# One transformer layer on one core: the first choice's expert rows are added to the residual by accumulating transfers instead of by VectorE

## What is computed

```python
def hier_moe(xn, w_rg, b_rg, w_re, b_re, w1, w3, w2):
    ...
    topv, topi = lax.top_k(lg_in, TOP_K_INNER)        # TOP_K_INNER = 2
    w_sel = jax.nn.softmax(topv, axis=-1) * p_sel[:, None]
    ...
    def expert_step(acc, inp):
        w1e, w3e, w2e, ge = inp
        hid = jax.nn.silu(t @ w1e) * (t @ w3e)
        return acc + ge[:, None] * (hid @ w2e), None
    ...

def block(x, mod, s_f0, s_b0, is_grid, p):
    ...
    x = x + g1 * m
    xn = rmsnorm(x, norm_ffn_g) * (1 + sc2) + sh2
    x = x + g2 * hier_moe(xn, w_rg, b_rg, w_re, b_re, w1, w3, w2)
    return x, s_f, s_b

y_prompt = rmsnorm(xp, final_norm_g)
y_sample = rmsnorm(xs, final_norm_g)
```

## Time and profile before

| | before |
|---|---|
| median of 3 runs (lowest to highest) | 709.08 us (708.93 to 710.7) |
| the profiled execution's own time | 708.17 us |
| its span | 706.4 us |
| TensorE busy | 597.8 us (85%) |
| VectorE busy | 311.9 us (44%) |
| ScalarE busy | 140.5 us (20%) |
| GpSimd busy | 145.4 us (21%) |
| start of the first load of the tail (L536) | 675.05 us |
| start of VectorE's first addition in the tail | 681.56 us |

### The profile page before, as it was taken

The page is one execution under the profiler, slowest core; times in us unless marked ns, Lnnn a source line. Parts: engine busy times, 40 slices in busy tenths (PEclk is TensorE's granted clock), DMA queues, the critical chain, the costliest instruction groups (busy, mean ns, idle before and its releaser), DMA issues.

```text
span 706.4 us, 8602 instructions
## 1 busy us (share of the span) xinstructions
PE 597.8 (85%) x3512; PEld 397.4 (56%) x3512; DVE 311.9 (44%) x619; ACT 140.5 (20%) x269; POOL 145.4 (21%) x112
## 2 busy tenths in 40 slices
PE   3799999999999899899999758898888788988800
PEld 3579999888888755444554435454444444544300
DVE  1432238432603246424677636554333434433347
ACT  5334522131322233211111120000000100100012
POOL 0133633333424000010000020232222222321200
PEclk9989999999999999999999559999999999999965
DMA  7985232031230697570006749999999999999484
GB/s 281 387 296 188 68 120 90 30 120 28 92 120 0 206 382 247 216 291 31 30 31 252 325 148 421 421 420 418 422 419 420 418 420 421 420 419 419 200 306 188
DMA packets 47463, 178.87 MB, mean 253 GB/s; under 512 B 5597, under 2 KB 5645, under 8 KB 34749
## 3 DMA queue, kind: packets, MB, share of 16 engines
q1 hardware_dynamic: 39128, 156.03, 55.9%
q0 software_dynamic: 7328, 19.63, 7.7%
q10 hardware_dynamic: 964, 2.63, 1.1%
HBM read 170.37 MB, written 14.19 MB: 261 GB/s over the span
## 4 chain that ended last, share of the span: by engine, by line
PE 60%; DMA 23%; DVE 7%; issue 3%; ACT 2%; POOL 2%; SPq 1%; POOLq 0%; ACTq 0%; DVEq 0%
DMA arena_cd<-expert_in_rows,idx 16%; PE bank L946 9%; PE bank L948 9%; PE bank L947 9%; PE bank L1116 9%; PE bank L1252 6%; DMA ring<-in_w_up_e 4%; PE bank L905 3%; POOL expert_out_rows L625 2%; DVE arena_ab L1334 2%; PE bank L1232 2%; DMA x<-in_x_sample 2%; PE bank L1133 2%; PE bank L1224 1%; DMA ring<-expert_out_rows 1%
## 5 line engine op out<-in xcount | busy, mean ns | idle before, releaser
L1232 PE MATMUL bank<-ring,arena_ab 128*64 128x256 f32 x416 | 96.1, 385 | 4.7 <-issue 2.1
L1236 PE MATMUL bank<-ring,arena_ab 128*64 128x256 f32 x416 | 96.2, 385 | 0.0
L1232 PEld LDWEIGHTS bank<-ring,arena_ab 128*64 128x64 f32 x416 | 57.6, 140 | 49.2 <-issue 20.5
L556 POOL TENSOR_TENSOR w_lo<-ring,w_hi 128x1024 fp32r<-128x1024 f32 x25 | 61.4, 2454 | 112.1 <-ACT w_hi L702 112.1
L625 POOL DMA_INDIRECT expert_out_rows<-arena_ab,row_out x32 | 40.6, 1269 | 191.7 <-DVE arena_ab L1334 191.7
L946 PE MATMUL bank<-xn_hi,w_hi 128*128 128x320 f32 x192 | 61.8, 322 | 3.0 <-DVE xn_lo L1334 2.9
L946 PE MATMUL bank<-w_hi,xn_hi 128*128 128x512 f32 x160 | 62.9, 393 | 0.0
L948 PE MATMUL bank<-w_hi,xn_lo 128*128 128x512 f32 x160 | 62.9, 393 | 0.0
L947 PE MATMUL bank<-w_lo,xn_hi 128*128 128x512 f32 x160 | 62.7, 392 | 0.0
L948 PE MATMUL bank<-xn_hi,w_lo 128*128 128x320 f32 x192 | 60.4, 315 | 0.0
L947 PE MATMUL bank<-xn_lo,w_hi 128*128 128x320 f32 x192 | 60.2, 313 | 0.0
(11 more groups left out here) (239 smaller groups left out, 930.3 us busy)
## 6 DMA issues: line engine op xcount, KB each, us to landing
ring<-in_w_gate_e SPq DMA_DIRECT2D x26, 1024.0 KB, 21.0
ring<-in_w_up_e SPq DMA_DIRECT2D x26, 1024.0 KB, 23.2
ring<-in_w_down_e SPq DMA_DIRECT2D x26, 1024.0 KB, 19.5
ring<-in_w_ada SPq DMA_DIRECT2D x11, 2048.0 KB, 11.2
ring<-in_w_in SPq DMA_DIRECT2D x6, 2048.0 KB, 8.2
arena_ab<-in_w_gate_e SPq DMA_DIRECT2D x6, 1024.0 KB, 21.4
arena_ab<-in_w_up_e SPq DMA_DIRECT2D x6, 1024.0 KB, 23.7
arena_ab<-in_w_down_e SPq DMA_DIRECT2D x6, 1024.0 KB, 19.7
```

What stands on the lines that cost most here:

```text
L556: pool.tensor_tensor(as_piece(w_lo[p_ % 2], p_), piece_of(w, p_), as_piece(w_hi[p_ % 2], p_), ALU.subtract).then_inc(w_lo_ready, 1)
L1232: pe.matmul(bank[2 + p_][0:BLK, 0:DE], lhs, w_gate(s)[:, kt, :], start=(kt == 0), stop=(kt == KT - 1))
L1236: last = pe.matmul(bank[2 + p_][BLK:2 * BLK, 0:DE], lhs, w_up(s)[:, kt, :], start=(kt == 0), stop=(kt == KT - 1))
```

## The change

The plain loads of the first choice's rows are taken out. In their place POOL issues, at the end of its program, five transfers that add the DRAM rows of the first choice to `x` where it lies (`accum_op=ALU.add`), tile by tile, after `y_all`. `got` shrinks to one piece for each tile. VectorE's `combine` waits for the load of the second choice and for the accumulating transfer of the same tile, and does one addition in place of two.

```diff
-        got = flat[:, 0:2 * NT * D].rearrange("p (t j n) -> p t j n", t=NT, j=2)
+        got = flat[:, 0:NT * D].rearrange("p (t n) -> p t n", t=NT)
...
+        first_sum = [sem(f"first_sum{t}") for t in range(NT)]
...
             sp.sem_inc(y_all, 1)
             for t in range(NT):
-                for j in range(2):
-                    sp.dma_start(got[:, t, j, :], y_rows[j * TOK + P * t:j * TOK + P * t + P, :]).then_inc(got_in[t], 16)
+                sp.dma_start(got[:, t, :], y_rows[TOK + P * t:TOK + P * t + P, :]).then_inc(got_in[t], 16)
...
                 pool.wait_ge(idx_ov_ready, 1)
+
+            pool.wait_ge(y_all, 1)
+            for t in range(NT):
+                pool.dma_start(x[:, t, :], y_rows[P * t:P * t + P, :], accum_op=ALU.add).then_inc(first_sum[t], 16)
...
             def combine(t):
 
-                g0, g1 = got[:, t, 0, :], got[:, t, 1, :]
-                dve.wait_ge(got_in[t], 32)
-                then(tt(g0, g0, g1, ALU.add))
-                tt(x[:, t, :], x[:, t, :], g0, ALU.add).then_inc(x2_ready[t], 1)
+                dve.wait_ge(got_in[t], 16)
+                dve.wait_ge(first_sum[t], 16)
+                tt(x[:, t, :], x[:, t, :], got[:, t, :], ALU.add).then_inc(x2_ready[t], 1)
```

## The result

| | before | changed |
|---|---|---|
| median of 9 runs each (lowest to highest) | 708.53 us (706.45 to 710.7) | 711.08 us (710.39 to 714.34) |
| ratio, 95% interval | | 1.0051 (1.0035 to 1.0067) |
| profiled execution, its span | 708.17, 706.4 us | 714.34, 712.5 us |
| start of SP's first load of the tail | 675.05 us | 678.64 us |
| from there to the start of c4's last addition | 21.2 us | 23.7 us |

The changed kernel is slower, by 0.5% by the ratio and by 0.4% by the two medians. Its profiled execution was the slowest of the nine: its tail begins 3.6 us later than that of the kernel before, and the change touches nothing ahead of the tail. The difference of the tails, 33.9 - 31.4 = 2.5 us, is also the difference of the two medians, 711.08 - 708.53 = 2.55.

The account below looks back on a forecast made before the run. VectorE's work was taken to bound the tail, with 4.7 us of transfer slack; dearer sums and a store move c4 from 696.26 to 699.2, +2.9 us on the 709.08 median: 712.0 us, range 705.4 to 718.3.

Parts of the forecast that it names:

- The bound: In the tail, VectorE's own work from c2 on sets the end; transfers have 4.7 us of slack.
- The gain: On VectorE, five additions go; only those of c2, c3 and c4 are on the path, at most 3.7 us.
- f = 2: Price of an accumulating transfer in plain loads, one per tile read; adds 6.3 us, last sum at 697.9; chance 0.36.
- POOL's issues at zero: On POOL, issuing five transfers takes 2.7 to 5.4 us from 675.05, ahead of the data, and costs nothing.
- the counting back: From the last sum at 697.9, pairs land 3.78 us apart, at 682.8, 686.6, 690.3, 694.1 and 697.9.
- The cover that was named: Five plain loads keep the transfer engines busy 6.3 us from 677.9, so late POOL issues cost little until about 684.
- A store among the sums, 1.26 us: n0's store moves its data while the last sums are moved, putting the last landing at 699.2 instead of 697.9.
- What c4 waits for: On VectorE, c4's remaining addition waits for the last accumulating transfer and starts at 699.2, against 696.26 before.
- the sum of +2.9 us: Net effect on the span: c4's addition starts at 699.2 in place of 696.26, slower by 0.4%.
- A free second read: Rival on the accumulating transfers: f = 1, the extra read costs nothing; -3.7 us, 705.4; chance 0.16.
- reads in turn: Rival on the accumulating transfers: f = 3, both reads and the write take turns; +9.2 us, 718.3; chance 0.15.
- the half-hidden one: Rival on the accumulating transfers: f = 1.5, second read half hidden; -0.3 to +1.0 us, 709.5; chance 0.33.

Follow-up runs that it names:

- the late kernels: Against the kernel before, POOL adds by transfer only tiles 3 and 4, after tile 1's loads (0.9974) or its first load (0.9972), or only tile 4, after tile 2's (0.9974).
- both choices added: Against the changed kernel, SP's loads and VectorE's additions are gone too; POOL's transfers add both choices' rows, a tile's second after its first has landed: ratio 1.0114.
- late sum for one tile: Against the kernel before, only tile 4 uses an adding transfer, issued once tile 2's loads have landed: 706.94 us, ratio 0.9974.
- Two batches of one kernel: Against the changed kernel, POOL's adding transfers became plain loads and VectorE adds twice again: 710.76 us, ratio 1.0035; run again 709.33 us, 1.0015.

## Why the prediction was right, point by point

- **The bound.** From c2 on VectorE's work set the end, and the last landing could move by 4.7 us before it held up the addition of c4 that stays. The change trades VectorE's time for transfer time. Right: the late kernels add 1.3 or 2.5 us of transfers and win, the changed kernel adds 6.3 and loses.
- **The gain** of at most 3.7 us, from the additions of c2, c3 and c4. Of these c2's went with the wait that now stands there, and 2.5 us of c3 and c4 came.
- **f = 2.** Right, and the step on which all depends: 3.78 to 3.84 us a pair in the changed kernel, packets that take 1.9 times as long, 202 and 211 GB/s for sums alone against 416, and two plain loads in place of each sum with the last landing within half a microsecond. The prediction's own formula for f gives about 1.85, since it takes off 1.26 us for a store that was not there; without that it gives 2.05. The Trainium skill's ratio of 1.93 ("Collectives: The Full Stack", on why ReduceScatter is half of AllGather) lies close to what this case shows (416 / 211 = 1.97, 416 / 202 = 2.06).
- **POOL's issues at zero.** The issuing came as worked out: five took 4.46 us (2.7 to 5.4), and were over at 678.88 + 4.46 = 683.3 (+4.7). But the pairs were late by 1.6 us, the first at +9.3 where 682.8 - 675.05 = +7.8 was worked out. The step that was off is the counting back: it let a tile of each queue move side by side to the very end, the last pair too. In fact SP's queue was a tile ahead, so the last sum moved almost alone, in 2.5 us and not 3.8, and the pairs before it lay 1.26 us later; the other 0.3 is the lateness of the last sum itself. How much of this POOL's queue adds is not separated. The cover that was named held for the transfers as a whole: without a store the last sum was reckoned at 697.9 - 675.05 = +22.9 and landed at +23.2.
- **A store among the sums, 1.26 us.** It did not delay them. n0's store was issued at 698.67 (+20.0), 3.1 us before the last sum landed, but its own landing came only 4.4 us later (703.1), behind that of the sum; in the kernel before every store took 2.6. In the view of the stores' line L541 it is the longest:

```profile
DMA to landing us min/median/max: 2.6/2.6/4.4
```

- **What c4 waits for.** The forecast had c4 wait for the last sum, with idle time ahead of it, at 699.2 - 675.05 = +24.1. In fact the sum was there half a microsecond before c4, and c4 followed n1, which followed c3, whose pair was 1.6 us later than reckoned. That the sum of +2.9 us comes so near to the 2.5 measured is in part luck: the 1.26 us of the store that did not come are nearly made up for by the last sum's 0.3 and the half microsecond by which n1 ends after that sum.
- **The rivals.** A free second read (705.4) and reads in turn (718.3) are both excluded by the pairs' spacing (3.8 us, where 2.5 and 5.04 were worked out), the half-hidden one by 202 to 211 GB/s (416 / 1.5 = 277).

## What to carry to other kernels

A transfer that adds to its destination moves the work from a compute engine to the transfer engines, at about the price of a second transfer. Compare the slack of both in the stretch in question: here the transfers had 4.7 us to spare, one or two tiles' worth of sums fitted in (0.997), five did not (1.005). Issue such transfers so that they do not push back loads that the chain waits for, and count what follows a wait on its engine to the very end of that engine's program.

## What was not expected of the hardware

- Five adding transfers of 128 rows of 4 KB, issued one behind the other, kept POOL for 4.46 us, 0.89 each, against 2.65 for five plain ones of the same shape. One by itself took 0.84 (both choices added) to 0.93 us (late sum for one tile).
- The queues of SP and POOL shared the engines by rows, whatever a row cost: from 685 to 695 us they moved 377 and 383 packets. That a sum's row costs two of the others slowed SP's loads as much as the sums, and the fifth of them landed at 699.7 (+21.1), although its own 512 KB tiles need only 6.3 us in all.
- Two batches of one kernel gave ratios of 1.0035 and 1.0015, while the two tails agreed within 0.2 us. But the tails scatter too: with the same first loads by SP alone, c0 started between +6.5 and +7.2 in five kernels. Differences of 0.2% are settled neither by one batch nor by one tail here; counting from c0 takes part of the scatter out.
